# Splitting three branches on GpSimd and moving four merge products in front of and between the steps of the recurrent mixer's norm

## The reference, cut to what matters

```python
y_a = short_conv_mixer(proj[..., SC_OFF:SB_OFF], sc_conv_w)
y_b = stick_breaking_attention(q, k, v)
y_c = rwkv7_mixer(proj[..., RW_OFF:SG_OFF], ...)     # state recurrence, then a norm over each head of 64
y_d = spatial_gating(proj[..., SG_OFF:GATE_OFF], ...)
merged = (gates[:, :, 0] * (y_a @ sc_out) + gates[:, :, 1] * (y_b @ sb_out)
          + gates[:, :, 2] * (y_c @ rw_out) + gates[:, :, 3] * (y_d @ sg_out))
return merged @ w_o
# in rwkv7_mixer, behind the recurrence:
mean = jnp.mean(y, axis=-1, keepdims=True)
var = jnp.mean(jnp.square(y - mean), axis=-1, keepdims=True)
y = ((y - mean) * lax.rsqrt(var + RW_GN_EPS)).reshape(bsz, t, RW_WIDTH)
y = y * gn_g + gn_b
y = (y + bonus) * g
```

## Time and profile before

| | us |
|---|---|
| median of 3 executions | 2590.64 |
| lowest, highest | 2589.44, 2611.47 |
| profiled execution, device time | 2590.81 |
| profiled execution, span | 2589.0 |
| PE busy | 2474.2 (96%) |
| POOL busy | 824.0 (32%) |
| DVE busy | 1053.5 (41%) |

### The profile page before, as it was taken

The page is one execution under the profiler, slowest core; times in us unless marked ns, Lnnn a source line. Parts: engine busy times, 40 slices in busy tenths (PEclk is TensorE's granted clock), DMA queues, the critical chain, the costliest instruction groups (busy, mean ns, idle before and its releaser), DMA issues.

```text
span 2589.0 us, 36011 instructions
## 1 busy us (share of the span) xinstructions
PE 2474.2 (96%) x15558; PEld 1959.1 (76%) x15558; DVE 1053.5 (41%) x1280; ACT 608.2 (23%) x901; POOL 824.0 (32%) x518
## 2 busy tenths in 40 slices
PE   7999999999999789999999999999899989979998
PEld 6887777777778677888888888887677866646676
DVE  5230222321475544254444444445333226675521
ACT  3101122222222212111111111112322015544410
POOL 4322332333232177523333333334632210131221
PEclk9999999999999999999999999999999989989999
DMA  5111322222100164211111111111113111000023
GB/s 190 47 42 58 96 82 74 73 82 75 52 14 4 62 207 139 70 45 49 49 49 49 49 49 49 49 49 41 44 38 107 48 57 46 2 8 1 1 64 115
DMA packets 194122, 156.89 MB, mean 61 GB/s; under 512 B 15674, under 2 KB 175649, under 8 KB 193738
## 3 DMA queue, kind: packets, MB, share of 16 engines
q1 hardware_dynamic: 193994, 155.00, 19.7%
HBM read 125.58 MB, written 29.40 MB: 60 GB/s over the span
## 4 chain that ended last, share of the span: by engine, by line
PE 85%; DVE 8%; POOL 3%; ACT 2%; issue 1%; DMA 0%; SPq 0%; POOLq 0%; DVEq 0%; ACTq 0%
PE gp L928 18%; PE gp L930 17%; PE gp L929 17%; PE sm L930 4%; PE sm L928 4%; PE sm L929 4%; PE sm L1582 2%; PE gp L1485 2%; PE gp L1501 2%; POOL merged L825 2%; PE sm L1518 2%; DVE att_s L2474 1%; PE sm L1090 1%; PE sm L1440 1%; PE sm L1069 1%
## 5 line engine op out<-in xcount | busy, mean ns | idle before, releaser
L928 PE MATMUL gp<-h_hi,w_hi 128*128 128x512 f32 x1600 | 638.3, 399 | 1.3 <-ACT k_sb L1670 1.3
L930 PE MATMUL gp<-h_hi,w_lo 128*128 128x512 f32 x1600 | 623.5, 390 | 0.0
L929 PE MATMUL gp<-h_lo,w_hi 128*128 128x512 f32 x1600 | 623.1, 389 | 0.0
L727 POOL CAST w_hi<-w_raw 128x1024 fp32r<-128x1024 f32 (+1 forms) x165 | 176.1, 1067 | 1130.8 <-PE gp L930 805.3
L729 POOL TENSOR_TENSOR w_lo<-w_raw,w_hi 128x1024 fp32r<-128x1024 f32 x173 | 432.7, 2501 | 105.2 <-ACT w_hi L1823 83.1
L928 PEld LDWEIGHTS gp<-h_hi,w_hi 128*128 128x128 f32 x1600 | 300.4, 188 | 84.0 <-issue 23.9
L929 PEld LDWEIGHTS gp<-h_lo,w_hi 128*128 128x128 f32 x1600 | 300.6, 188 | 64.5 <-issue 4.5
L930 PEld LDWEIGHTS gp<-h_hi,w_lo 128*128 128x128 f32 x1600 | 300.3, 188 | 63.9
L2100 DVE TENSOR_TENSOR_SCAN sb_run<-sb_keep,ones_row 128x128 f32<-128x128 f32 (+7 forms) x32 | 77.1, 2449 | 318.1 <-POOL sb_keep L774 318.1
L928 PE MATMUL sm<-h_hi,w_hi 128*128 128x512 f32 x352 | 136.9, 389 | 0.0
L929 PE MATMUL sm<-h_lo,w_hi 128*128 128x512 f32 x352 | 136.9, 389 | 0.0
(11 more groups left out here) (477 smaller groups left out, 4033.0 us busy)
## 6 DMA issues: line engine op xcount, KB each, us to landing
w_raw<-in_w_in SPq DMA_DIRECT2D x79, 512.0 KB, 4.4
w_raw<-in_w_up SPq DMA_DIRECT2D x44, 512.0 KB, 3.9
gates_spill<-gate_out SPq DMA_DIRECT2D x32, 512.0 KB, 3.1
gate_in<-gates_spill SPq DMA_DIRECT2D x32, 512.0 KB, 4.3
w_raw<-in_w_down SPq DMA_DIRECT2D x22, 512.0 KB, 3.3
x_back<-x_spill SPq DMA_DIRECT2D x16, 512.0 KB, 4.0
x_tok<-in_x SPq DMA_DIRECT2D x8, 512.0 KB, 8.1
x_spill<-x_t SPq DMA_DIRECT2D x1, 4096.0 KB, 15.0
```

What stands on the lines that cost most here:

```text
L727: pool.tensor_copy(w_hi[:, t % 2, 0:n], w_raw[:, t % 2, 0:n]).then_inc(s["w_high"], 1)
L928: pe.matmul(o, wh, hi[:, k0 + k, c], start=(k == 0), stop=False)
L929: pe.matmul(o, wh, lo[:, low[k] if low else k0 + k, c], start=False, stop=False)
L930: mm = pe.matmul(o, wl, hi[:, k0 + k, c], start=False, stop=(k == n - 1))
```

## The change

Three parts, and the order that goes with them.

The splits: POOL casts and subtracts y_a (within the tenth round of the inversion), y_d (behind the rounds, its second tile after the product xa of the second `ft`) and y_b (at the end of the chain). ACT and DVE keep y_c alone. The tiles of `y_hi`, `y_lo`, `gate_in`, `gated` and `y_rstd` get new places, and y_a's and y_d's own space is no longer waited for.

The products: (0, 0) is made in two halves ahead of the chain, into banks 2 and 3 of `sm`, and gated before the chain. For that the chain's state sums share two banks, and DVE copies both `ft` in one instruction. (0, 1) is made between the centring sums and the variance sums, (1, 0) between these and `rk_g`, and DVE gates both before it norms. (1, 1) follows `rk_g` and is gated behind the norm. MERGE_ORDER is changed to suit.

The rest: SP loads the gates and the weight tiles T_BR + 2 and T_BR + 3 earlier, each behind a stage of the mixer; ACT casts the weight tile T_BR + 1 before the chain ends; both `normed` follow one another, and the two tiles of y_c are split one by one between gated products.

```diff
+EARLY = 1
+MERGE_ORDER = [(0, 0), (0, 1), (1, 0), (1, 1), (0, 2), (1, 2), (0, 3), (1, 3)] + \
     [(d, n) for d in range(2, KT) for n in range(4)]
...
+            if P_BR <= p < P_BR + EARLY:
+                return sm[:, 2:4, :].rearrange("p a b -> p (a b)")
...
+        def gate_place(d, n):
+            return gate_first if n == 0 and d < 2 else gate_in[n]
+
+        def state_place(ch):
+            u = ch // 2 % 4
+            return sm[:, ch % 2, :].rearrange("p (f u c) -> p f u c", f=2, u=4)[:, :, u, :]
...
# SP
-            sp.wait_ge(s["y_split"], 4)
...
+            sp.wait_ge(s["rk_post"], 3)
+            load_gate(0, 0)
+            load_gate(0, 1)
+            load_weights(T_BR + 2)
+            sp.wait_ge(s["rk_post"], 10)
+            load_gate(0, 2)
+            load_gate(1, 0)
+            load_gate(1, 1)
+            sp.wait_ge(s["rk_y"], 1)
+            load_gate(0, 3)
+            load_weights(T_BR + 3)
+            load_gate(1, 2)
+            load_gate(1, 3)
+            sp.wait_ge(s["rk_y_done"], 2)
+            for d in range(2, KT):
                 for n in range(4):
+                    load_gate(d, n)
                 load_weights(T_BR + 2 + d)
...
# POOL
+            def split_branch(n, y):
+                for ft in range(2):
+                    j = 2 * n + ft
+                    if j == 3:
+                        pool.wait_ge(s["rk_post"], 7)
+                    wait.after(pool.tensor_copy(y_hi[j][:, :], y[:, ft, :]))
+                    pool.tensor_tensor(y_lo[j][:, :], y[:, ft, :], y_hi[j][:, :].bitcast(F32), ALU.subtract) \
+                        .then_inc(s["y_split"], 1)
...
+                    if z == 10:
+                        pool.wait_ge(s["sc_done"], 1)
+                        pool.wait_ge(s["rk_post"], 3)
+                        split_branch(0, y_a)
...
+            pool.wait_ge(s["rk_lv"], 10)
+            pool.wait_ge(s["sg_done"], 4)
+            split_branch(1, y_d)
             split_weights(T_BR + 1)
             for q, (d, n) in enumerate(MERGE_ORDER):
+                if q == EARLY:
+                    pool.wait_ge(s["rk_y"], 1)
+                    split_branch(2, y_b)
...
# PE
             rk_rounds(1, rk_post_0)
+            merge(0, 0, (0,))
             pe.wait_ge(s["rk_x_added"], 20)
...
             rk_post("q", 1, 0)
+            merge(0, 0, (1,))
             pe.wait_ge(s["rk_post1"], 6)
...
             for ft in range(2):
+                if ft == 0:
+                    merge(0, 1)
                 pe.wait_ge(s["rk_yc_sb"], ft + 1)
                 head_sum(yc_sq[ft], 2 * ft, "rk_var")
-            merge(0, 0)
+            merge(1, 0)
...
# ACT
+            high_weights(T_BR + 1)
             act.wait_ge(s["rk_y"], 1)
...
-            y_high(0, y_a)
...
-            y_high(1, y_d)
-            y_high(2, y_b)
-            act.wait_ge(s["rk_y_done"], 2)
-            y_high(3, y_c)
+            for ft in range(2):
+                act.wait_ge(s["rk_y_done"], ft + 1)
+                act.copy(y_hi[6 + ft][:, :], y_c[:, ft, :]).then_inc(s["high"], 1)
...
# DVE
+            gate_product(0)
             for ch in range(NCH - 1):
                 dve.wait_ge(s["rk_chain"], ch + 1)
-                for ft in range(2):
-                    ins = dve.tensor_copy(s_all[:, ch + 1, ft, :],
-                                          sm[:, 2 * ft + ch % 2, C * (ch // 2):C * (ch // 2) + C])
-                ins.then_inc(s["rk_state"], 1)
+                dve.tensor_copy(s_all[:, ch + 1, :, :], state_place(ch)).then_inc(s["rk_state"], 1)
...
+            gate_product(1)
+            gate_product(2)
             for ft in range(2):
                 normed(ft)
-            y_low(2, y_b)
-            gate_product(0)
-            gate_product(1)
-            y_low(3, y_c)
-            for q in range(2, 4 * KT):
+            gate_product(3)
+            for ft in range(2):
+                y_low(ft)
+                gate_product(4 + ft)
+            for q in range(6, 4 * KT):
                 gate_product(q)
```

More of the change, by code:

```diff
@@ L1273, in rk_rounds, with merge @@
                     beside(2 * (n - 1) + 1)
+            def merge(d, n, halves=(0, 1)):
+                t, q = T_BR + d, MERGE_ORDER.index((d, n))
+                p = P_BR + q
+                if halves[0] == 0:
+                    pe.wait_ge(s["w_split"], t + 1)
+                    pe.wait_ge(s[f"p_free{p % 2}"], frees_before(p))
+                    if 0 < q < EARLY:
+                        pe.wait_ge(s[f"p_free{(p - 1) % 2}"], frees_before(p - 1) + 1)
+                for half in halves:
+                    c = slice(HALF * half, HALF * half + HALF)
+                    o = slot(p)[:, c]
+                    for k in range(2):
+                        if d == 0 and half == 0:
+                            wait("y_split")
+                        wh, wl = ring(t, 256 * n + P * k, 256 * n + P * k + P)
+                        hi, lo = y_hi[2 * n + k], y_lo[2 * n + k]
+                        pe.matmul(o, wh, hi[:, c], start=(k == 0), stop=False)
+                        pe.matmul(o, wh, lo[:, c], start=False, stop=False)
+                        mm = pe.matmul(o, wl, hi[:, c], start=False, stop=(k == 1))
+                if halves[-1] == 1:
+                    mm.then_inc(s["p_ready"], 1)
             def rk_local(ch):
@@ L2319, in gate_product, with y_low, normed @@
                     merge_low(d - 1)
-            y_low(1, y_d)
+            gate_product(0)
+            for ch in range(NCH - 1):
+                dve.wait_ge(s["rk_chain"], ch + 1)
+                dve.tensor_copy(s_all[:, ch + 1, :, :], state_place(ch)).then_inc(s["rk_state"], 1)
+            def y_low(ft):
+                wait("high")
+                dve.tensor_tensor(y_lo[6 + ft][:, :], y_c[:, ft, :], y_hi[6 + ft][:, :].bitcast(F32),
+                                  ALU.subtract).then_inc(s["y_split"], 1)
+            for ft in range(2):
+                dve.wait_ge(s["rk_yc_sq"], ft + 1)
+                dve.tensor_copy(yc[ft], sm[:, 2 * ft:2 * ft + 2, :].rearrange("p a b -> p (a b)")) \
+                    .then_inc(s["rk_yc_sb"], 1)
+            dve.wait_ge(s["rk_yc_sb"], 2)
+            def normed(ft):
+                dve.wait_ge(s["rk_rstd"], ft + 1)
+                wait.after(dve.tensor_tensor(yc[ft], yc[ft], y_rstd[ft][:, :], ALU.mult))
+                wait.after(dve.scalar_tensor_tensor(yc[ft], yc[ft], pcol("gn_g", ft), rk_vb[ft], ALU.mult, ALU.add))
+                dve.wait_ge(s["rk_g"], ft + 1)
+                dve.tensor_tensor(y_c[:, ft, :], yc[ft], sm[:, 2 * ft:2 * ft + 2, :].rearrange("p a b -> p (a b)"),
+                                  ALU.mult).then_inc(s["rk_y_done"], 1)
+            gate_product(1)
+            gate_product(2)
             for ft in range(2):
                 normed(ft)
-            y_low(2, y_b)
-            gate_product(0)
-            gate_product(1)
-            y_low(3, y_c)
-            for q in range(2, 4 * KT):
+            gate_product(3)
+            for ft in range(2):
+                y_low(ft)
+                gate_product(4 + ft)
+            for q in range(6, 4 * KT):
                 gate_product(q)
```

81 lines of the change are left out of this document (30 added, 51 removed).

## The result

| | before | after |
|---|---|---|
| median, us | 2591.36 | 2583.18 |
| lowest, highest | 2588.4, 2611.47 | 2580.34, 2586.92 |
| executions | 20 | 20 |
| profiled execution, device time | 2590.81 | 2582.85 |
| profiled execution, span | 2589.0 | 2581.1 |

The ratio is 0.9949, 95% interval 0.993 to 0.9967; the medians alone stand at 0.9968, 8.2 us apart. Five of the 20 executions of before lie near 2610 us and none of after does (of the experiments' executions 4 of 10 in the third, 1 of 10 in the eighth and 1 of 6 in the twelfth lie 13 to 20 us above the others), so the difference of the profiled executions, 8.0 us, is what the text explains. The forecast was 2582.0.

What follows compares the result with a forecast made beforehand. PE is busy nearly throughout, so only the stretch where it stands still, ahead of (2, 0), can give much. 41.0 - 50.7 + 0.7 = -9.0, +0.4 makes -8.6: 2582.0 us; own range 2579 to 2585, whole range 2576 to 2590.

Steps and rivals of the forecast that it cites:

- The number to work out was (2, 0) behind the chain.: Start of PE's product (2, 0) behind the recurrent chain's end: 41.0 us forecast, against 50.7 before.
- m_lo(0) getting in first: Ahead of (2, 0): DVE's m_lo(0) precedes w_lo about half the time, ending w_lo at 41.1 instead of 40.0; 41.0 taken.
- One low part held back: Behind the norm: y_c's low parts alternate with POOL's adds, second low part 27.2 to 28.3 us behind the chain.
- DMAs cost nothing … over a nearly idle queue: Gates and tiles asked for earlier cost nothing, except (1, 3)'s gate, landing 36.5 us behind the chain.
- The insertion: Product (0, 0) in two halves ahead of the chain: chain ends 0.7 us later, bounds 0.3 and 2.5.
- The four switches: Tile-size switches between 64x64 and 128x128 matmuls around the two halves: charged nothing; up to 0.9 us worse by the skill.
- The copy is not on the path: One state copy for two in the recurrent chain: 0 us gained, bounds -2 us and 0.
- The two rivals on the chain: Recurrent steps 0.14 us shorter (2579, chance 0.10), or longer through shared banks (2594, 0.10 together with product not ahead).
- y_a's split ahead of the product: POOL's y_a split in the inversion: last level from about 818.8 to 821.2, PE reads at 830.8, 9.6 us spare.
- The rival that the product isn't ahead: PE waits for y_a's split inside the inversion; needs POOL 16 us late; slower, chance 0.10 shared with longer steps.
- DVE's partners with one input in PSUM keep their 1.22: DVE operations with one PSUM input keep 1.22 us beside POOL's work, so y_d's split costs 0.
- Lower clock +0.4: PE's wait ahead of (2, 0) grows from 5.7 to about 8 us, lower clock lasts longer behind it: +0.4 us.

Runs made afterwards that it cites:

- the third: Changed kernel with only product (0, 0)'s gate tile loaded early, (0, 1)'s gate and weight tile T_BR + 2 later; median 2583.22 us, ratio 0.9976.
- the eighth: Changed kernel with one early gate load, T_BR + 2 behind the gates, and own places for (1, 2)'s and (1, 3)'s gate tiles; median 2581.6 us, ratio 0.9954.
- the twelfth: Changed kernel with one early load, own places for two gate tiles, and next weight tile's cast and subtraction ahead of d's last add; median 2569.35 us, ratio 0.9888.
- The seventh run: Changed kernel with own places for the gate tiles of (1, 2) and (1, 3), loaded right behind the chain; 2584.32 us.
- the fourth run: Changed kernel with the chain's state copied by two DVE instructions again, one per `ft`, banks still shared; 2586.17 us.

## Why the prediction was right, point by point

- *The number to work out was (2, 0) behind the chain.* 41.3 against 41.0 (before 50.7). Norm 14.9 behind the chain (forecast 15.1). m_hi 909.90, w_hi 910.85, w_lo 912.06: 36.8, 37.7 and 38.9, each of which the forecast had 1.2 us earlier. The seventh run, which takes away the wait for (1, 2)'s gate tile, gives 1.2 us back. It had taken 1 us for m_lo(0) getting in first, which didn't happen. Right in sum, by two misses of opposite sign, which is luck.
- *One low part held back.* Forecast as an alternation; the rows show one 2.29 and one 1.22. Right.
- *"DMAs cost nothing … over a nearly idle queue"* is the step that failed. SP's three loads in a row, beside PE's 64x64 matmuls, cost PE 1.85 us of idling and a stretch at 0.50: the round 3.1 us longer. I had looked at the queue and at the data's due times, not at what else the DMA engines serve: the q8 record due near 814.0 starts at 815.9. The round lies ahead of the stretch from 830 in which I had placed the change. Without it the chain would have ended about where before's does (third run, 870.39; forecast 871.4). The same sentence took (1, 3)'s gate as the only one that is late; (1, 2)'s is as well (2.51 us, had the pattern), and the seventh run prices both at 1.2 us together.
- *The insertion* is right in size. The first half's matmuls start at 836.82 and PE's next product at 838.41, the second from 844.57 to the local products at 846.15. Read against the same neighbours in the earlier trace rows, that is 0.74 and 0.16, 0.9 in sum where 0.7 was forecast. From this round's zr to the chain's end it takes 47.2 to 47.7 us in the five kernels without the insertion and 48.1 to 48.9 in the nine with it, which says the same. The four switches were taken at nothing on the strength of the earlier trace rows. By the drain that the Trainium skill states for a change of tiling mode (TensorEngine Tiling (Array Packing), Key Properties), the prediction's estimate had up to 0.9 us on top; some 0.2 is there.
- *The copy is not on the path*: shown by the fourth run, steps of 1.79 us with one copy and with two. Before, with four banks, had 1.79 as well, so sharing the banks costs nothing either. The two rivals on the chain (shorter or longer steps) are out.
- *y_a's split ahead of the product*: m_lv from 817.18, forecast 818.8; not late. The rival that the product isn't ahead falls.
- *DVE's partners with one input in PSUM keep their 1.22*: the row at 918.69 had POOL's subtraction w_lo beside it and not an add, as the forecast read it; in after gated (0, 2) keeps 1.22 beside POOL's adds (897.72). Right.
- *Lower clock +0.4* had the wrong sign. PE's wait ahead of (2, 0) grew from 5.58 to 6.42 us, yet the clock of 0.50 behind it lasts about 3.3 us and not longer than before's 4.4; and the 5.20 us at 0.50 behind the old hole are gone, which the forecast had counted in the distance and not as clock. From (2, 0) at -6.9 the loop, period still 12.1 to 12.2, made -7.7 of it by m_lo(7); some 0.5 of these 0.8 us are the shorter low clock.

Sum, as it went: -9.4 behind the chain, +2.4 ahead of it, about -0.9 behind (2, 0): -7.9. The forecast had -9.7, +0.7, +0.4: -8.6. Three misses, +0.3, +1.7 and -1.3, in part cancelled, and the +2.4 would be 3.6 had the round begun where before's does: that much is luck. Its 2582.0 stands 1.2 us from the median.

What stays open: a proof that the late fetch is what stops PE (its records fit in all fourteen kernels, but no run delayed a fetch by itself), why the clock falls behind the chain's 1.10 us hole in some executions and not in others, why the round near 816 begins up to 2.3 us apart in kernels alike up to there, and the part of about 1 us that the eighth run lost inside the loop. Apart from 3, 8 and 12, each experiment is one execution, so differences under about 1 us between them rest on their rows alone.

## What to carry to other kernels

A load that no one waits for can still cost time: 1.5 MB beside a stretch of short matmuls stopped PE for about 2 us, and 0.5 MB at a time didn't, so spread early loads. Count a moved piece of work twice, once for its own time and once for what it now meets: the product ahead of the chain was worth 2.7 us as work and 2.6 as order. And when a stretch ends in a loop with a period of its own, look at the loop first: a cast and a subtraction moved ahead there gave some 12 us, half as much again as the whole change.

## What the hardware showed beside that

- PE's idle time without a releaser behind bulk loads: 1.4 to 2.5 us in the nine kernels with 1.5 MB landing between about 810 and 819, 0.6 with 1 MB, none there with 0.5 MB and 0.3 in the kernel before. The records of 16 KB in the instruction queue q8 are 5.2 to 6.0 us apart there in these nine, 4.3 with 1 MB and 3.5 to 4.0 in the other four, in a stretch in which a matmul starts about every 26 ns (76 in 2 us).
- The granted clock behind the chain's hole of 1.10 us, the same in every kernel, was 0.50 for some 3 us in six kernels (sums 5.16 to 5.40 us) and 1.00 in the other eight (3.70).
- An operation of DVE on two SBUF tiles and an add of POOL run one behind the other, for both DVE operations seen here: 3.29 us for the norm's scalar_tensor_tensor instead of 1.28, 2.29 for a low part instead of 1.22, 4.55 for two low parts instead of 2.35. The Trainium skill (SBUF — State Buffer, Who interferes with whom) says that a DVE instruction with two SBUF inputs contends with a GpSimd instruction that reads SBUF, and the trace agrees.
